# Experts taken in order of load, the four smallest with the high and low parts of their tokens in one stationary operand

## The reference

```python
def moe_swiglu(h, w_router, w_gate, w_up, w_down):
    logits = (h @ w_router).astype(jnp.float32)
    top_v, top_i = lax.top_k(logits, TOP_K)          # TOP_K = 2
    top_w = jax.nn.softmax(top_v, axis=-1)
    gates = jnp.sum(jax.nn.one_hot(top_i, N_EXPERTS) * top_w[..., None], axis=-2)
    y = jnp.zeros_like(h)
    for e in range(N_EXPERTS):                        # 8
        y = y + gates[..., e:e + 1] * swiglu(h, w_gate[e], w_up[e], w_down[e])
    return y
```

## Time and profile before

| | |
|---|---|
| runs | 1430.37 us median of 3 (1429.91 to 1433.1) |
| profiled execution, its span from first to last instruction | 1428.0 us; the profile gives no other time for it, and the median stands 2.4 us above the span |
| busy shares: PE, weight loading (PEld), DVE, ACT | 98%, 82%, 78%, 65% |
| one expert in the steady stage | 119.13 us |
| DMA share in tenths, 40 equal slices of the span | `9744455555533999999999999999999999999992` |
| granted TensorE clock, mean | 0.997 |

### The profile page before, as it was taken

One profiled execution on the slowest core, in us unless ns is written; L12 is line 12 of the kernel. 1 busy time (PEld: TensorE's weight loads), 2 busy tenths in 40 slices (PEclk: granted clock), 3 DMA queues, 4 the chain that ended last, 5 costly groups with the idle time before them and its releaser, 6 DMA issues.

```text
span 1428.0 us, 16665 instructions
## 1 busy us (share of the span) xinstructions
PE 1401.6 (98%) x6886; PEld 1177.1 (82%) x6886; DVE 1110.8 (78%) x838; ACT 934.2 (65%) x723; POOL 44.1 (3%) x48
## 2 busy tenths in 40 slices
PE   9999999999999999999999999999999999999997
PEld 7886788887988888888888888888888888888885
DVE  4786644556465988898888989888888898988896
ACT  3665444345354777777777777777777777777774
POOL 0000000000010000000000000000000000001000
PEclk9999999999999999999999999999999999999999
DMA  9744455555533999999999999999999999999992
GB/s 310 223 166 148 141 199 177 177 190 183 202 119 118 370 382 362 385 365 386 367 399 384 352 400 376 369 384 369 393 364 397 388 346 402 380 369 384 414 369 121
DMA packets 136848, 440.17 MB, mean 308 GB/s; under 512 B 11472, under 2 KB 28864, under 8 KB 121024
## 3 DMA queue, kind: packets, MB, share of 16 engines
q1 hardware_dynamic: 130688, 424.24, 80.2%
q0 software_dynamic: 3600, 13.12, 2.4%
q10 hardware_dynamic: 2480, 1.69, 0.4%
HBM read 433.25 MB, written 5.78 MB: 307 GB/s over the span
## 4 chain that ended last, share of the span: by engine, by line
PE 89%; DVE 6%; ACT 2%; DMA 2%; issue 1%; ACTq 0%; DVEq 0%
PE ps L1749 28%; PE ps L1751 28%; PE ps L1750 28%; PE ps L2284 2%; DVE lo L1136 2%; DMA wr<-in_od_w_router_dram 1%; DVE work L1162 1%; ACT hi L727 1%; PE ps L2204 0%; DMA x<-in_x_dram 0%; PE ps L2045 0%; PE ps L1940 0%; DVE work L1325 0%; DVE negmax L1313 0%; DMA normed_tokens<-work 0%
## 5 line engine op out<-in xcount | busy, mean ns | idle before, releaser
L1136 DVE TENSOR_TENSOR lo<-raw,hi 128x2048 fp32r<-128x2048 f32 (+1 forms) x403 | 904.4, 2284 | 108.5 <-ACT hi L727 106.4
L727 ACT ACTIVATE hi<-raw 128x2048 fp32r<-128x2048 f32 (+1 forms) x403 | 770.8, 1916 | 247.4 <-PE ps L1751 236.9
L1749 PE MATMUL ps<-hi,xT_hi 128*128 128x512 f32 (+1 forms) x1200 | 471.2, 393 | 5.4 <-DVE lo L1136 2.8
L1751 PE MATMUL ps<-hi,xT_lo 128*128 128x512 f32 (+1 forms) x1200 | 465.0, 388 | 0.0
L1750 PE MATMUL ps<-lo,xT_hi 128*128 128x512 f32 (+1 forms) x1200 | 464.4, 387 | 0.0
L1749 PEld LDWEIGHTS ps<-hi,xT_hi 128*128 128x128 f32 x1200 | 226.4, 189 | 53.4 <-DVE lo L1136 4.7
L1751 PEld LDWEIGHTS ps<-hi,xT_lo 128*128 128x128 f32 x1200 | 225.7, 188 | 46.7
L1750 PEld LDWEIGHTS ps<-lo,xT_hi 128*128 128x128 f32 x1200 | 226.1, 188 | 43.5
L1749 PE MATMUL ps<-hi,hT_hi 128*128 128x512 f32 x520 | 204.1, 392 | 0.0
L1751 PE MATMUL ps<-hi,hT_lo 128*128 128x512 f32 x520 | 202.6, 390 | 0.0
L1750 PE MATMUL ps<-lo,hT_hi 128*128 128x512 f32 x520 | 202.4, 389 | 0.0
(11 more groups left out here) (278 smaller groups left out, 718.4 us busy)
## 6 DMA issues: line engine op xcount, KB each, us to landing
raw<-in_od_w_gate_dram SPq DMA_DIRECT2D x112, 1024.0 KB, 7.8
raw<-in_od_w_up_dram SPq DMA_DIRECT2D x112, 1024.0 KB, 8.0
raw<-in_od_w_down_dram SPq DMA_DIRECT2D x112, 1024.0 KB, 7.5
raw<-in_od_w_qkv_dram SPq DMA_DIRECT2D x12, 1024.0 KB, 5.2
raw<-in_ev_w_gate_dram SPq DMA_DIRECT2D x11, 1024.0 KB, 5.2
raw<-in_ev_w_up_dram SPq DMA_DIRECT2D x11, 1024.0 KB, 5.1
raw<-in_ev_w_down_dram SPq DMA_DIRECT2D x11, 1024.0 KB, 5.0
raw<-in_ev_w_in_dram SPq DMA_DIRECT2D x4, 1024.0 KB, 10.9
```

The costliest lines, as they stand in the source:

```text
L727: act.activation(unit(hi, n), unit(raw, n), ACT.Copy).then_inc(hi_ready, 1)
L1136: dve.tensor_tensor(unit(lo, n), unit(raw, n), unit(hi, n).bitcast(F32), ALU.subtract)\
L1749: pe.matmul(out, s_hi, m_hi, start=start, stop=False, skip_group_check=True)
L1751: return pe.matmul(out, s_lo, m_hi, start=False, stop=stop, skip_group_check=True)
```

## The change

The experts 1 to 7 are sorted by their number of tokens on the chip. The three largest come first, behind expert 0, with the products as before; the four smallest come last. The branch now asks that expert 0 and the largest have at most 128 tokens and the fourth largest of the seven at most 64. In the four small experts (`SMALL`) slots 0 to 63 hold the high part and slots 64 to 127 the low part of the same 64 tokens: one stationary operand for both, and two products (`both`) in place of three. Gate and up results come out in two halves, are copied by ACT (`keep_gate`, `keep_up`), and `turn` multiplies them with a matrix `fold64`, which transposes and adds the halves; Silu, the multiplication and the next split then work on 128x256. The two halves of a result are stored one after the other, the second one adding into the first.

```diff
+SMALL = [4, 5, 6, 7]
+LARGE = [1, 2, 3]
...
-            return eng.value_load(most_i[0:1, 0:1], min_val=0, max_val=SEQ) <= P
+            return eng.value_load(most_i[0:1, 0:1], min_val=0, max_val=NE * (SEQ + HALF) + NE - 1) <= MOST
...
             for e in range(NE):
+                gate_w, up_w, down_w = moe_gate[0], moe_up[0], moe_down[0]
+                if e:
+                    sp.wait_ge(order_ready, 1)
+                    expert = sp.value_load(order_i[0:1, e - 1:e], min_val=1, max_val=NE - 1)
+                    gate_w, up_w, down_w = (w[bass.ds(expert, 1)][0] for w in (moe_gate, moe_up, moe_down))
...
+                    n = HALF if e in SMALL else P
+                    pool.indirect_dma_start(rows[0:n], None, normed_d,
+                                            bass.IndirectOffsetOnAxis(ap=picked[0:n], axis=0)).then_inc(rows_landed, 16)
                     pool.wait_ge(y_copied, e)
+                    kept = result_d[row_at[e - 1]:row_at[e], :]
+                    if e - 1 in SMALL:
+                        pool.dma_start(kept, y_out[0:HALF]).then_inc(y_stored, 16)
+                        pool.wait_ge(y_stored, stores_before(e) - 16)
+                        pool.dma_start(kept, y_out[HALF:P], accum_op=ALU.add).then_inc(y_stored, 16)
...
+            def keep_gate(e, c):
+                w = MOE_CHUNKS[c][1]
+                act.wait_ge(units_used, first_of(e) + UP_AT[c])
+                act.wait_ge(g_h_done, NCH * e + c)
+                act.wait_ge(g_hT_done, NSUB * e + SUBS[c][0])
+                act.activation(work[:, 0, 0:w], ps[:, 4:4 + w // W, :].rearrange("p a n -> p (a n)"), ACT.Copy)\
+                    .then_inc(g_silu_done, 1)
...
+            def turned_silu(e, s):
+                act.wait_ge(g_hT_done, NSUB * e + s + 1)
+                if small_subs(e, s) >= 2:
+                    act.wait_ge(t_h_done, small_subs(e, s) - 1)
+                act.activation(swish[:, sub_slot(s)], ps[:, 7, 0:SEQ], ACT.Silu).then_inc(t_silu_done, 1)
+            def turned_high(e, s):
+                act.wait_ge(t_h_done, small_subs(e, s) + 1)
+                act.activation(hT_both(s)[:, :, 0:HALF],
+                               h_turned[:, sub_slot(s)].rearrange("p (j q) -> p j q", q=HALF), ACT.Copy)\
+                    .then_inc(g_hT_hi_ready, 1)
...
+            def turned_multiply(e, s):
+                dve.wait_ge(t_silu_done, small_subs(e, s) + 1)
+                dve.tensor_tensor(h_turned[:, sub_slot(s)], swish[:, sub_slot(s)], ps[:, 7, SEQ:2 * SEQ], ALU.mult)\
+                    .then_inc(t_h_done, 1)
+            def turned_low(e, s):
+                dve.wait_ge(g_hT_hi_ready, NSUB * e + s + 1)
+                dve.tensor_tensor(hT_both(s)[:, :, HALF:P],
+                                  h_turned[:, sub_slot(s)].rearrange("p (j q) -> p j q", q=HALF),
+                                  hT_both(s)[:, :, 0:HALF].bitcast(F32), ALU.subtract).then_inc(g_hT_ready, 1)
...
+            def in_order(to, of):
+                link(dve.tensor_copy(to[:, :, 0:1], of[:, :, 0:1]))
+                link(dve.tensor_tensor(spread[:], stands_at[:].unsqueeze(1).broadcast_to([P, T, NE - 1, NE - 1]),
+                                       of[:, :, 1:NE].unsqueeze(2).broadcast_to([P, T, NE - 1, NE - 1]), ALU.mult))
+                link(dve.tensor_reduce(to[:, :, 1:NE], spread[:], AX.X, ALU.add))
+            def order_experts():
...
+                dve.tensor_copy(order_i[0:1, 0:NE - 1], order[0:1, 0:NE - 1]).then_inc(order_ready, 1)
+                in_order(spick, rpick)
+                in_order(splace, rplace)
...
-            link(dve.tensor_copy(rcount[:], ps[:, 6, 32:40]))
-            link(dve.tensor_reduce(most[:], rcount[0:1, :], AX.X, ALU.max))
+            dve.tensor_scalar(load_limit[:, 0:1], ps[:, 6, 32:33], float(NE), None, ALU.mult)
+            link(dve.scalar_tensor_tensor(out=load_key[:, 0:NE - 1], in0=ps[:, 6, 33:40], scalar=float(NE),
+                                          in1=iota[:, 1:NE], op0=ALU.mult, op1=ALU.add))
+            link(dve.max(by_load[:], load_key[:]))
+            dve.tensor_copy(load_limit[:, 1:2], by_load[:, 0:1])
+            link(dve.tensor_scalar(load_limit[:, 2:3], by_load[:, len(LARGE):len(LARGE) + 1], float(NE * HALF), None,
+                                   ALU.add))
+            link(dve.tensor_reduce(most[:], load_limit[0:1, 0:3], AX.X, ALU.max))
...
                 gathered_low(0)
+                order_experts()
                 gates_soft()
...
+            def both(out, s_both, m_hi, m_lo, start, stop):
+                pe.matmul(out, s_both, m_hi, start=start, stop=False, skip_group_check=True)
+                return pe.matmul(out, s_both, m_lo, start=False, stop=stop, skip_group_check=True)
...
+            def turn(e, s, c):
+                pe.wait_ge(g_silu_done, NCH * e + c + 1)
+                pe.wait_ge(g_h_done, NCH * e + c + 1)
+                if s:
+                    pe.wait_ge(t_h_done, small_subs(e, s))
+                else:
+                    pe.wait_ge(g_hT_ready, NSUB * e)
+                f = W * (s - SUBS[c][0])
+                for part in range(2):
+                    for j in range(4):
+                        first = SEQ * part + HALF * j
+                        ins = pe.matmul(ps[:, 7, first:first + HALF], work[:, part, f + j:f + W:4], fold64[:],
+                                        start=True, stop=True)
+                ins.then_inc(g_hT_done, 1)
```

## The result

The forecast was wrong. The changed kernel takes 1433.28 us (median of 20 runs, 1428.29 to 1440.72), the kernel before 1430.14 us (median of 20 runs, 1427.96 to 1433.1) beside it. The ratio is 1.0028 [1.0017, 1.0038]: slightly slower, where I had forecast 1397.2 us and a range of 1374 to 1421. The profiled execution took 1428.29 us with a span of 1426.5 us; it is the fastest of the twenty, so everything read from it flatters the change by some 5 us.

What follows compares the result with a forecast made beforehand. PE was taken to bound each expert at 119.13 us, with transfers at 112 us replacing it in the four small ones. A gain of 35.9 us less 2.7 us of sorting gave 1397.2 us, range 1374 to 1421.

Steps and rivals of the forecast that it cites:

- 56 x 0.23 = 12.9 us: PE in a small expert: 56 true fp32 products of 64 columns replace 28 transposes, at 0.23 us each.
- 90.6: PE's total work in one small expert, in us: weight products 76.2, turns 12.9, gather and pick 1.5.
- some 0.7 us late, seven times an expert, 5 us: Small experts: DVE's multiplication waits for ACT's Silu behind a split waiting for a landing; 103.6 + 5 stays under 112.
- Rival 2: Small experts: DVE's hand-offs cost 1.8 us idle per turn, not 0.7; 116 us an expert, 1412 us; chance 0.10.
- the credit of the ring: Start of expert 4: five loads already issued, the fifth just landing, so transfers have 163 units left, 434.7 us.
- The path is taken: Branch to the small form: fourth largest expert has 62 tokens, under 64; the rival that it isn't taken had 0.01.
- Transfers at 112 us: Small experts: loads and stores of 44.8 MB replace PE as the bound, between 107.8 and 114.5 us an expert.
- the ring and the tail: Last four experts: 434.7 us for 163 remaining units, then 6.0 us for the last unit through ACT, DVE, PE.
- DVE at 103.6: VectorE's work in one small expert, in us, including 42 differences at 96.0; close behind the transfers.
- the lower edge of my range: Forecast range's 1374 us end: 7 us below the fast transfer bound, for a full queue at 425 GB/s.
- Rival 1: Small experts: transfers already at their limit, share 0.99 at 380 GB/s; 117.9 us an expert, 1420 us; chance 0.11.
- Rival 3: Small experts: gaps in PE drop its clock to 1.2 GHz; half and half 124 us an expert, 1452 us; chance 0.08.

Runs made afterwards that it cites:

- e11: e5 with two more products of 512 columns per unit, adding zeros, in the small experts: 1408.18 us, ratio 0.9848 to the kernel before.
- e5: Changed kernel, values right, with ACT's copies reading PSUM at a step of four so that turns read contiguous columns: 1399.88 us, ratio 0.9777 to the kernel before.
- e8: e6 without fetching and adding the earlier experts' results in the last expert (output lacks them): 1394.89 us, ratio 0.9753 to the kernel before.
- e10: e5 with only half of each unit of the small experts loaded, the rest old data: 1360.43 us, ratio 0.9513 to the kernel before.
- e4: Changed kernel with sorting, register loads and new branch condition, but no expert in the small form: 1433.87 us, against 1430.61 for the kernel before.
- e3: Changed kernel with only half of each unit of the small experts loaded, the rest old data: 1426.46 us, ratio 0.9964 to the kernel before.
- e13: Changed kernel with two idle products of 512 columns at the head of each turn, meant to hold PE's clock: 1446.66 us, ratio 1.0106 to the kernel before.
- e9: e5 with the eight products of each turn issued twice, so turns are long but contiguous: 1422.5 us, ratio 0.9942 to the kernel before.
- e6: Changed kernel with hidden columns in blocks of 128 for all experts, every transpose contiguous, down loads in 4 KB runs: 1402.13 us, ratio 0.9799 to the kernel before.
- e1: Changed kernel with turns reading 128 columns side by side instead of every fourth (values wrong): 1400.65 us, ratio 0.9781 to the kernel before.
- e12: e5 with six small experts instead of four: 1385.7 us, ratio 0.969 to the kernel before.

## Why the prediction was wrong

**The step that failed** is the term "56 x 0.23 = 12.9 us": seven turns take 7 x 3.52 = 24.6 us. I had taken the price from products whose stationary operand is contiguous and asked of the moving side only how many columns it has. PE then needs 90.6 + 11.7 = 102.3 us. That alone is still under 112. What makes it decisive is where the turn stands; e11 has more work on PE elsewhere and shorter periods. There the second figure fails, "some 0.7 us late, seven times an expert, 5 us" for DVE. DVE's multiplication is queued behind ACT's Silu and that behind the whole turn; DVE has no other work in its list before it, and the splits behind it wait too. Measured are 14.3 us in seven waits in the kernel after, and 3.9 us in five waits in e5 with the short turn. In e5 ACT waits for a turn for only 1.3 us an expert, and the rest is what the prediction named, a Silu queued behind a split that waits for a landing. In the kernel after ACT waits 14.6 us for the turns. So the 0.7, cause and size, was right for a turn of 1.8 us; for one of 3.5 another wait ends last.

**Rival 2 is what came,** with the wait and the price that it was given: 1.8 us a turn and 116 us an expert, against 2.0 and 113.8 to 116.5. That the price fits is partly luck, as the rival named no longer turn. I had put it at 0.10 and at 1412 us. Its time was too low, since I let it keep the credit of the ring: a period that DVE holds gains nothing from loads in flight. Experts 4 to 6 took 346.0 of the 473.0 us, and the last one 127.0, 11 more than 116. There DVE has four additions of results on it, 5.1 us, and waits 6.4 us for ACT's splits instead of 1.3; what the results cost was measured only in e8, beside short turns (7.2 us). The step from the profiled 1428.29 us to the median of 1433.28 goes with a lower clock, below.

**What held.** The path is taken. Transfers at 112 us: e5 shows 107.0, 110.0 and 111.7, at a share of 1.02 and 406 GB/s, and e10 shows that they are its bound. With the ring and the tail the prediction has 434.7 + 6.0 = 440.7 us for four experts; PE's last weight product in e5 ends at 1388.3, 442.2 us after its expert 4 begins. The Trainium skill's 358 GB/s (DMA: Bandwidth & Descriptors, Specifications) stays below what this core sustained over a whole expert, 406. DVE at 103.6 was somewhat high: it is full at 100.2, as its long operations start 2.20 us apart ((19.89 - 2.29) / 8) though each is recorded with 2.29. ACT's 95 was near (91). `order_experts` took 2.4 us for 2.7, e4 3.3 in all. At the lower edge of my range a sum is off: a rate of 425 GB/s would give 9 us below the fast bound, not 7; nothing hangs on it. Rival 1 is excluded for this kernel by e3, though its sign, a share of 1.01 at 385 GB/s, is in the profile: a share near 1 means full engines only if the period moves when bytes are taken away.

**Rival 3 in part.** The clock doesn't fall for long: 0.97 over experts 4 to 6. But it does fall, and behind turns. Window and timeline of PE after one that ended at 1131:

```profile
1130.00:1135.00 5.00, 5.00 (x17) 4.14 (x17) 3.44 (x5) 3.28 (x5) 0.00 (x0) 0.66 1.03 412
```

```profile
1131.01 0.47 PE L2493 MATMUL ps<-hi,xT_hi 128*128 128x512 f32 x1
1131.32 0.56 PE L2494 MATMUL ps<-lo,xT_hi 128*128 128x512 f32 x1
1131.67 0.63 PE L2493 MATMUL ps<-hi,xT_hi 128*128 128x512 f32 x1
1132.10 0.63 PE L2494 MATMUL ps<-lo,xT_hi 128*128 128x512 f32 x1
```

Products start 0.43 us apart, the 1.2 GHz level, right behind 3.5 us in which PE loaded strided operands. From 943 to 1290 us the timeline has six such stretches, of six or seven products each, and each stands right behind one of the 21 turns. In e13 there are eleven, of four to eight products, again each behind a turn. In e9, whose turns are as long but contiguous, there is none, and the window's clock reads 1.00. e5 has two, both over 6 us behind a turn; before the first PE was busy for 5.17 of 7.3 us. So turns are not the only occasion. Six stretches of seven products, 0.43 - 0.23 us longer each, make 8.4 us (an estimate); the three periods of the kernel after sum to 346.0 us and e9's to 340.0, 6.0 less.

The twenty runs go with it: 1428.29 us at a mean clock of 0.986, 1433.16 at 0.982, 1440.72 at 0.977, 12.4 us for 0.009; the kernel before stands at 0.997. So the 10.8 us between e9 and the kernel after fit the clock by size, and in these traces it falls behind strided turns and not behind contiguous ones of the same length. That is seen side by side and not shown as the cause of the 10.8 us: no run holds the clock up with the strided turns in place (e13 was to and didn't), and why it falls behind some turns and not behind others stays open.

## What to carry to other kernels

Price both operands of a product, and look for a weight load with the same access pattern in the trace that you have: here a step of four fp32 made it 327 ns instead of 192 and cost a 2.2% gain, which a free rearrangement in a copy on ACT gave back. The transposes of the kernel before, with the same step, already showed 205 ns instead of 139. That row doesn't give the 327, but it says that the contiguous price can't be used. An operation in a chain of hand-offs counts with its full length for every engine that works through a fixed list behind it, even where its own engine has room. A DMA share of 1 is a bound only if halving the bytes moves the period.

## What was not expected of the hardware

- LDWEIGHTS of 128x128 fp32 takes 191 ns contiguous (e5) and 327 ns with a step of 16 bytes (the kernel after). A recorded pass of load and product then takes 0.22 us instead of 0.11 (3.52 and 1.73 us for 16). In a transpose the same step makes the load 205 ns instead of 139 and costs a large expert 0.2 us for 28 of them (e6).
- TensorE's clock can fall to 1.2 GHz behind a stretch in which it was never idle: six times behind turns of strided loads in the kernel after, never behind contiguous turns of the same length in e9 (both from 943 to 1290 us).
- ACT reads PSUM with a step of four fp32 at no cost: 1014 ns for 1024 columns in e5, against 1020 contiguous in the kernel after.
- One core sustained 402 to 406 GB/s over 347 us (e1, e5, e6, e12).
